# One product later: when VectorE drains a product in the two seven-product output stages

## What is computed

```
def swiglu(h, w_in, w_out):                      # w_in 1024 x 5632, w_out 2816 x 1024
    a, b = jnp.split(h @ w_in, 2, axis=-1)
    return (jax.nn.silu(a) * b) @ w_out
...
x_lat = x_lat + 0.5 * mod_l[:, 8] * swiglu(modulate(x_lat, ...), ffn_b_in[i], ffn_b_out[i])
x_ctx = x_ctx + 0.5 * mod_c[8] * swiglu(modulate(x_ctx, ...), ffn_b_in[i], ffn_b_out[i])
```

## Time and profile before

| | |
|---|---|
| median of 3 runs | 2458.72 us (2457.57 to 2459.1) |
| the profiled execution: time | 2454.37 us |
| the profiled execution: span from first to last instruction | 2452.6 us |
| TensorE matmul busy | 2379.8 us, 97% of the span |
| VectorE busy | 1571.4 us, 64% |
| ScalarE busy | 1155.8 us, 47% |
| GpSimd busy | 256.8 us, 10% |
| mean granted TensorE clock | 0.997 of full speed |
| first output stage, from its first matmul | 948.05 us |
| second output stage, from its first matmul | 1300.79 us |

### The profile page before, as it was taken

One profiled execution on the slowest core, in us unless ns is written; L12 is line 12 of the kernel. 1 busy time (PEld: TensorE's weight loads), 2 busy tenths in 40 slices (PEclk: granted clock), 3 DMA queues, 4 the chain that ended last, 5 costly groups with the idle time before them and its releaser, 6 DMA issues.

```text
span 2452.6 us, 47341 instructions
## 1 busy us (share of the span) xinstructions
PE 2379.8 (97%) x18669; PEld 1643.4 (67%) x18669; DVE 1571.4 (64%) x2258; ACT 1155.8 (47%) x1744; POOL 256.8 (10%) x255
## 2 busy tenths in 40 slices
PE   6999999998999999999999999999999999999999
PEld 4444444454544446854447858888888889878888
DVE  5556542566576667876658757467766765786774
ACT  4444422335454453455434454345555545565554
POOL 1124001004110000100000232011100000010001
PEclk9999999999999999999999999999999999999999
DMA  9896632231046654365544444137886676544675
GB/s 325 197 209 210 185 109 69 86 103 35 18 150 193 205 190 117 89 207 189 180 126 124 121 130 138 53 104 204 238 237 178 200 218 173 148 138 126 192 212 140
DMA packets 621670, 384.33 MB, mean 157 GB/s; under 512 B 11211, under 2 KB 580912, under 8 KB 621416
## 3 DMA queue, kind: packets, MB, share of 16 engines
q1 hardware_dynamic: 617000, 370.06, 51.0%
q0 software_dynamic: 4112, 11.44, 2.9%
q10 hardware_dynamic: 432, 1.04, 0.1%
HBM read 381.41 MB, written 1.08 MB: 156 GB/s over the span
## 4 chain that ended last, share of the span: by engine, by line
PE 84%; DVE 9%; DMA 2%; ACT 2%; issue 1%; SPq 1%; DVEq 0%; ACTq 0%
PE PS L872 21%; PE PS L874 21%; PE PS L873 21%; PE PS L963 2%; DMA arena<-in_w_mod 2%; PE PS L964 2%; PE PS L965 2%; DVE WL L2042 2%; DVE arena L2392 1%; PE PS L789 1%; DVE XL L2398 1%; ACT WH L1456 1%; PE PS L1249 1%; SPq L639 1%; PE PS L1321 1%
## 5 line engine op out<-in xcount | busy, mean ns | idle before, releaser
L872 PE MATMUL PS<-XH,WH 128*128 128x512 f16 (+2 forms) x2912 | 938.8, 322 | 14.7 <-DVE XL L2398 8.2
L873 PE MATMUL PS<-XL,WH 128*128 128x512 f16 (+2 forms) x2912 | 938.2, 322 | 0.0
L874 PE MATMUL PS<-XH,WL 128*128 128x512 f16 (+2 forms) x2912 | 937.9, 322 | 0.0
L1456 ACT ACTIVATE WH<-W 128x1024 f16<-128x1024 f32 (+1 forms) x530 | 572.1, 1112 | 530.9 <-PE PS L874 427.4
L2042 DVE SCALAR_TENSOR_TENSOR WL<-W,WH 128x1024 f16<-128x1024 f32 (+1 forms) x488 | 614.7, 1288 | 136.8 <-ACT WH L1456 136.2
L872 PEld LDWEIGHTS PS<-XH,WH 128*128 128x128 f16 x2912 | 285.4, 98 | 203.1 <-DVE XL L2398 16.1
L874 PEld LDWEIGHTS PS<-XH,WL 128*128 128x128 f16 x2912 | 285.2, 98 | 177.5 <-issue 1.4
L873 PEld LDWEIGHTS PS<-XL,WH 128*128 128x128 f16 x2912 | 285.2, 98 | 169.6 <-issue 1.1
L1456 ACT ACTIVATE arena<-arena 128x1024 f16<-128x1024 f32 (+4 forms) x344 | 228.9, 702 | 109.8 <-DMA arena<-in_w_mod 46.2
L872 PE MATMUL PS<-arena,WH 128*128 128x256 f16 (+1 forms) x832 | 245.5, 295 | 2.4 <-DVE WL L2042 2.4
L874 PE MATMUL PS<-arena,WL 128*128 128x256 f16 (+1 forms) x832 | 245.5, 295 | 0.0
(11 more groups left out here) (354 smaller groups left out, 2807.1 us busy)
## 6 DMA issues: line engine op xcount, KB each, us to landing
arena<-in_w_mod SPq DMA_DIRECT2D x72, 1024.0 KB, 7.9
W<-in_ffn_a_in SPq DMA_DIRECT2D x88, 512.0 KB, 5.2
W<-in_ffn_b_in SPq DMA_DIRECT2D x88, 512.0 KB, 4.7
W<-in_w_ffn_gu SPq DMA_DIRECT2D x88, 512.0 KB, 4.3
W<-in_ret_in SPq DMA_DIRECT2D x48, 512.0 KB, 4.7
W<-in_w_ffn_down SPq DMA_DIRECT2D x32, 704.0 KB, 5.7
W<-in_ffn_a_out SPq DMA_DIRECT2D x28, 704.0 KB, 5.9
W<-in_ffn_b_out SPq DMA_DIRECT2D x28, 704.0 KB, 5.7
```

Source lines behind the costliest of these rows:

```text
L872: mm(dst, wh, xh, start=(kp == 0 and c == 0), stop=False, skip_group_check=True)
L873: mm(dst, wh, xl, start=False, stop=False, skip_group_check=True)
L874: return mm(dst, wl, xh, start=False, stop=(kp == g["parts"] - 1 and c == kc - 1), skip_group_check=True)
L1456: return act.activation(dst, src, ACT.Copy, scale=scale)
```

## The change

In VectorE's list for the two output stages, iteration f drains products up to f-4 before the split of f, instead of up to f-3. At f = 4 that is product 0 alone instead of products 0 and 1; from then on each iteration drains one product, one older than before. At the end, products 24 to 27 are drained after the last split instead of 25 to 27. No instruction is added or removed.

```
             def dve_fast(g, after, between={}):
                 drained_to = 0
                 for f in range(3, 4 * FORMS):
-                    while f > 3 and drained_to <= f - 3:
+                    while f > 3 and drained_to <= f - 4:
                         fast_drain(g, drained_to)
                         drained_to += 1
                     fast_rest(g, f)
```

## The result

The change makes the kernel slower, by 0.3%: 2465.74 us median (2462.74 to 2467.95, 6 runs) for 2457.86 (2457.24 to 2459.1, 6 runs) of the kernel before, ratio 1.0032 with a 95% interval of 1.0019 to 1.0045, 7.9 us. Timed once more beside the kernel before on one chip it was 2464.93 for 2458.37, ratio 1.0025 (1.0014 to 1.0036), 6.6 us. The forecast was 2464.8, slower by 6.1.

A forecast was written before the change was run, and what follows sets the result against it. TensorE's matmuls and holes were taken to bound the output stages, with VectorE and ScalarE a second chain hardly shorter. 2 x 3.06 + 0.3 - 0.34 = 6.1 us slower, from 2458.72 to 2464.8 us; range 2461.5 to 2471.0.

The forecast's parts named there:

- The second step: Both output stages: drain 7 moves behind split 10 and sum 10, so product 9 starts 3.06 us later in each.
- The first step: At f = 4 only drain 0 runs ahead of the split; VectorE's chain runs 0.40 us earlier from there on.
- The third step: Quarters three and four: VectorE gets ahead; products 16 and 23 only 0.08 us late, 0.3 in all; stage 1's 0.34 goes.
- the present 0.34 at product 16: Stage 1: product 16's existing 0.34 us delay, waiting for drain 14, was to go, covered by 3.06 us of slack.
- The clock: TensorE's 3.05 us hole before product 9: clock fall costed at nothing; if it falls, about 3.0 us a stage.
- the second rival: The clock falls in the new hole of both stages: 12.1 us slower, 2470.8 us; chance 0.12.
- No stall: Rival: VectorE runs ahead and drain 7 still comes in time; only 0.7 us of holes go, 2458.0 us; chance 0.10.
- The hole in every quarter: Rival: VectorE can't get ahead after product 9, product 16 is 2.67 us late; 16.5 us slower, 2475.2; chance 0.05.
- Nothing outside the stages: Rival: an effect outside the stages, such as weights loaded sooner, makes it faster by more than 0.2%; chance 0.03.

The follow-up runs named there:

- e1: The kernel before with only drain 7 moved, from ahead of split 10 to ahead of split 11, in both stages: 2467.75 us for 2458.11, ratio 1.0039.
- e2: The change, but drain 7 keeps its old place ahead of split 10: 2463.07 us for 2458.11 of the kernel before, ratio 1.0019.
- e8: The change with drain 7 kept in its old place and stage 1's small step moved from f = 12 to f = 27: 2459.26 us for 2458.62 before.
- e9: The change itself, timed and profiled again beside the kernel before on one chip: 2464.93 us for 2458.37, ratio 1.0025.
- e5: Every drain one product later than in the change, up to f-5 ahead of split f: 2480.57 us for 2458.62 of the kernel before, ratio 1.0093.

## Why the prediction was right, and where not

**The second step, drain 7's new place, was right in place and size.** Forecast 3.06 us a stage; measured 3.07 in both, with drain 7, split 10 and sum 10 in the order and at the times given. e1 shows that this move alone makes the holes. The reason given, that VectorE's chain is not paced by TensorE up to there, is what e2 and e8 bear out: drains may come a product later at next to no cost where the chain is on time, and cost microseconds where it is late.

**The first step**, 0.40 us from f = 4 on, was right: split 10, with one drain ahead of it in both kernels, starts at 982.25, which is 980.42 less the 1.83, where the earlier trace rows give 980.82. e1 brings drain 7 to the same place in another way, so e1 doesn't measure this term.

**The third step was right in its mechanism and off in one term.** In stage 2 split 14 starts 1.40 us after ScalarE (1350.57 to 1351.97), and products 16 and 23 are 0.08 late each, as forecast. In stage 1 I wrote that the present 0.34 at product 16 goes. It stayed: 1011.05 to 1011.49, a step of 0.44 where the gapless one is 0.11. ScalarE's start on matrices 13 and 14, then VectorE's splits 13 and 14, with drain 10 between them:

```profile
991.57 0.21 ACT L1754 ACTIVATE lgt<-lgt 128x8 f32<-128x8 f32 x1
991.68 1.36 ACT L1456 ACTIVATE WH<-W 128x1408 f16<-128x1408 f32 x1
993.34 1.38 ACT L1456 ACTIVATE WH<-W 128x1408 f16<-128x1408 f32 x1 [0.30 <-PE PS L965]
```

```profile
993.08 1.62 DVE L2095 SCALAR_TENSOR_TENSOR WL<-W,WH 128x1408 f16<-128x1408 f32 x1 [0.23 <-ACT WH L1456]
994.62 0.48 DVE L2114 SCALAR_TENSOR_TENSOR X<-PS,modT,X 128x256 f32<-128x256 f32 x1
995.01 1.62 DVE L2095 SCALAR_TENSOR_TENSOR WL<-W,WH 128x1408 f16<-128x1408 f32 x1
```

Split 14 starts 1.67 us after ScalarE, not 1.41. The small step of f = 12 still holds split 13, by way of ScalarE: its last operation on ScalarE (991.57) stands ahead of the rounding of matrix 13, for which split 13 waits. So the slack of 3.06 us was some 0.26 too short, and 0.08 + 0.26 is the 0.34 that stayed at product 16. In e9, where the fallen clock makes product 9 another 1.7 us longer, product 16 is only 0.09 late. So the holes cost 3.14 + 3.22 = 6.4 us, not 6.1.

**The clock was mis-sized.** It was costed at nothing, since the idle time of 3.05 us lay nearest to the 2.92 after which the earlier trace rows show 1.00. It fell in seven of eight such holes. The row itself was the luck of one execution: behind the same 2.92 us the clock is lower in seven of the thirteen profiles, that of the change among them. A single profile of the kernel before couldn't tell this. The rule of the Trainium skill that the prediction set against the row (TensorE: Matmul & The Clock Gate, "HAM oscillation - how this bites in real kernels") pointed the better way: a wait between bursts of matmuls may find the clock at its lower level. That single holes of this length do it, in seven of eight cases, is what the runs here add.

The price of a fall was below the forecast 3.0 each time, 1.4 to 2.9 us. So the second rival is partly what happened, on top of the forecast: 6.4 us of holes, and in the two profiled executions of the change 1.7 and 4.3 us by the clock. The timed 7.9 and 6.6 leave 1.5 and 0.2 for it, less than these profiles; how often the clock falls in runs without a profile can't be read here and stays open. That the time came out so near the forecast is in part luck, as the clock's term was missing from the sum.

**The rivals.** "No stall" fell with drain 7's time. "The hole in every quarter" fell: products 16 and 23 wait 0.1 to 0.3 us, not 2.67. Nothing outside the stages gave time back; the stretch between them is the same to 0.01 us.

## What to carry to other kernels

When one engine serves another from a list, the lag of an item says little; what matters is which item the bound engine waits for next and what stands ahead of it in the list, so follow the list over a whole period, with its slowest stretch (here the small step and the split beside GpSimd's adds), before a step is moved. A second engine that is 84% busy over a stage can still set the pace in its first third, here up to product 9 of 28. A hole in TensorE's stream should be priced with the clock that may fall in it, and one profile doesn't tell whether it falls: look for the same wait in several. A few matmuls of constants kept the clock here; they must end before the hole does, and the time they saved (5.8 us over before, for 6.6 and 7.9) lies within the scatter of the runs.

## What the hardware showed that was not expected

Idle times of 3.06 to 3.16 us in a dense stream of matmuls were followed by the lower clock in seven of eight cases, for 1.4 to 2.9 us of loss. One of 2.92 us in another stage, in code that all runs share, was followed by it in seven of thirteen profiles, and one of 2.74 us (before the start at 591.37 in the kernel before) in eleven of thirteen, though the profile of the kernel before shows it at neither. The eight holes of e5 with 1.85 to 2.44 us of idle time show no fall. Eight operations of 8 columns on VectorE, with two exchanges with ScalarE and a table load of 1.28 us there, take 2.5 us, more than a split of 1408 columns. And that split takes 1.6 us by itself but mostly 2.3, and up to 2.7, when GpSimd adds squares at the time, while the sum of the same width beside it stays at 1.62. It is not always the split that is slow: in e2 split 11 of stage 2 took 1.62 us beside an addition of GpSimd that took 3.93, where it takes 2.4 in e8 beside a split of 2.69.
